# Next layer's adaptive blocks among the mix blocks, semaphores cleared in two parts, norms tile by tile, 64-row pairs side by side

## Chip, cores and metric

The kernel runs on one core of a Trainium2 chip. The metric is the device time in microseconds (us); the median of three runs of the kernel before is 3287.51 us.

## What is computed

The reference is a decoder trunk of two layers for 256 tokens of width 1024. For each layer:

```
ada = silu(c) @ w_ada + b_ada -> shift1, scale1, gate1, shift2, scale2, gate2
h = rms_norm(x) * (1 + scale1) + shift1
z = h @ w_in                     # columns for three mixers and the merge gates
m = sig(gA)*attention(z) + sig(gB)*conformer_conv(z) + sig(gC)*rwkv7(z)
x = x + (1 + gate1) * (m @ w_out)
h = rms_norm(x) * (1 + scale2) + shift2
x = x + (1 + gate2) * peer(h)    # 16384 experts, 16 taken for each token and head
```

and at the end `rms_norm(x)` with a gain. The kernel computes peer() densely: the scores of all 16384 experts, a gate for each (zero for those not taken), and the product of gate times activation with all the rows of v.

## The kernel before

Everything is held transposed, feature by token: x and h are eight tiles of 128 features by 256 tokens (`xT`, `hT`). Weights come as blocks of 1 MB, one after the other, into a ring of four slots (`ring`, `SLOTS`), always in the order of the array `stream`. SyncE's queue (SP) issues nearly all loads from one instruction stream, written out by hand, in which a load of block n waits until block n - 4 has been used up. What SP issues later in this stream waits behind what it issues earlier.

A layer is a loop body (`Fori`), the same program for both layers. Its stages are:

1. Eight adaptive blocks (the columns for shift1 and scale1). VectorE (DVE) reduces each with two tensor_tensor_reduce (L1181) against silu(c). The other 16 adaptive blocks lie further on in the stream, between blocks that TensorE (PE) uses (`late_ada`).
2. The first norm: ScalarE (ACT) squares all of xT in one instruction (L894), PE sums with eight matmuls against ones (`norm_sum`, L553), ACT takes the root (L896), DVE takes the reciprocal (L1133), scales eight tiles (L1136) and adds the shift to eight tiles (L1142).
3. The projection z, each weight split in a high and a low part (`zw_hi` by ACT at L916, `zw_lo` by DVE at L1220), three matmuls for one (L547).
4. Attention, convolution and RWKV. In RWKV, `pairs` (L712, L713) multiplies 64-row operands: a head has 64 rows, and two heads share the 128 partitions. A head's two matmuls (Bh, Kh) follow each other, then come those of the next head. They fill the time in which PE would wait for ACT's copies between the steps of a chain (L758, L769, L788).
5. `W_OUT`, the projection of the merged mixers (L532), all engines meet, then the second norm as in 2.
6. Scores: 64 blocks of u (`PEER`), split in high and low parts, 24 matmuls for each of 128 chunks of experts (L835). The activations are stored to DRAM row by row (`store_act`, L448), as are the gates.
7. Mix: 64 blocks of v, two chunks each. For chunk c, ACT copies the high part of v (`v_high`, L1075, four deep), DVE subtracts for the low part (`v_low`, L1570), and `weigh(c)` multiplies the gate row by the activation row (L1676) and splits the product in high and low (L1680, L1682), two deep. PE does twelve matmuls a chunk (L856) and needs v's low part and the split of the product. In DVE's stream v_low(c+3) and weigh(c+2) take turns.
8. End: ACT and DVE copy the sums out of PSUM, PE transposes them (L881), DVE adds to xT (L1706), the engines meet, and POOL clears all 138 semaphores while the others wait (`layer_end`). Then the next pass of the loop begins with loads of the parameters `prm`, of c and of the first four blocks.

The place that matters for stage 7 is SP's loop. In the kernel before it reads:

```
for q in range(SLOTS, PAIRS):
    sp.wait_ge(S["v_lo"], 2 * (q - SLOTS) + 2)
    load(PEER + PAIRS + q)
    for c in (2 * q - 6, 2 * q - 5):
        if c >= ROWS_DEEP:
            load_rows(c)
```

So when v_low of both chunks of block q - 4 is done (chunks up to 2q - 7), SP loads block q, and then the gate and activation rows of chunks 2q - 6 and 2q - 5, 128 KB each (`load_rows`: L455, L456). DVE waits for the rows of a chunk at L1676.

## Time and profile before

| | us |
|---|---|
| median of three runs (3279.75 to 3289.98) | 3287.51 |
| the profiled execution, its own time | 3290.19 |
| its span, from the first to the last instruction | 3288.4 |
| PE busy in it | 2962.9 (90%) |
| DVE busy | 2314.4 (70%) |
| ACT busy | 1114.9 (34%) |
| POOL busy | 99.0 (3%) |
| HBM traffic, mean over the span | 186 GB/s |

A row of the profile names the engine, the line of the kernel, the operation, and the tiles written and read (out<-in). In square brackets stands how long the engine was idle before, and what ended that wait. L12 is line 12 of the kernel before. Views in order of time begin with the start and the duration in us; a row with "xN" covers N instructions. A matmul in f32 shows as two records. The mean granted clock of TensorE is 0.954 of full speed.

### The profile page before, as it was taken

To read this page: it belongs to the slowest core of one execution; us is meant where nothing else is said; L and a number is where in the kernel's file an instruction comes from. 1 tells how busy PE (TensorE), PEld (TensorE's weight loads), DVE (VectorE), ACT (ScalarE), POOL (GpSimd) and SP (SyncE) were. 2 spreads that over 40 slices of the span, in tenths; PEclk is the share of its full clock that TensorE was granted. 3 is DMA by queue.
4 is the path that set the end of the run, shared out by engine and by line. 5 is a ranking of instruction groups with operands and counts; after the bars stand their busy time and mean duration, and the time that the engine had idled before them with its cause. 6 is when DMAs were issued, how large, how long until landed. Compare 5 with 4: busy or idle time off the path is not lost. (4 is left out here: it accounts for less than half of the span.)

```text
span 3288.4 us, 49870 instructions
## 1 busy us (share of the span) xinstructions
PE 2962.9 (90%) x19180; PEld 2662.7 (81%) x19180; DVE 2314.4 (70%) x4571; ACT 1114.9 (34%) x1532; POOL 99.0 (3%) x120
## 2 busy tenths in 40 slices
PE   4997898879999999999769879897899999999996
PEld 4996787768999998887569858776789999988885
DVE  6888564545887847888578895645468868478885
ACT  3434321201444444333234342211024444433332
POOL 0000003200000000000000000031000000000000
PEclk8998999989999999999979989998999999999998
DMA  6552340053666688887465424300546575978783
GB/s 243 184 188 77 119 170 8 29 208 116 207 208 213 215 295 283 283 280 277 142 238 188 156 77 159 129 8 32 211 139 213 189 249 190 320 266 284 278 281 109
DMA packets 268992, 613.57 MB, mean 187 GB/s; under 512 B 45520, under 2 KB 210000, under 8 KB 211664
## 3 DMA queue, kind: packets, MB, share of 16 engines
q1 hardware_dynamic: 203152, 576.79, 49.9%
q10 hardware_dynamic: 65600, 33.55, 3.4%
q8 instruction: 154, 2.52, 0.3%
q14 instruction: 86, 0.70, 0.1%
HBM read 540.53 MB, written 69.73 MB: 186 GB/s over the span
## 5 line engine op out<-in xcount | busy, mean ns | idle before, releaser
L835 PE MATMUL ps<-h_hi,u_hi 128*128 128x256 f32 x2048 | 592.0, 289 | 34.6 <-DVE u_lo L1563 34.2
L835 PE MATMUL ps<-h_hi,u_lo 128*128 128x256 f32 x2048 | 582.4, 284 | 0.0
L835 PE MATMUL ps<-h_lo,u_hi 128*128 128x256 f32 x2048 | 582.2, 284 | 0.0
L1563 DVE TENSOR_TENSOR u_lo<-ring,u_hi 128x1024 fp32r<-128x1024 f32 x256 | 311.7, 1220 | 252.4 <-ACT u_hi L1067 251.9
L835 PEld LDWEIGHTS ps<-h_hi,u_hi 128*128 128x128 f32 x2048 | 395.5, 193 | 42.9 <-DVE u_lo L1563 36.0
L1075 ACT ACTIVATE v_hi<-ring 128x1024 fp32r<-128x1024 f32 x256 | 271.3, 1062 | 437.8 <-PE ps L856 437.8
L835 PEld LDWEIGHTS ps<-h_lo,u_hi 128*128 128x128 f32 x2048 | 395.5, 193 | 0.0
L835 PEld LDWEIGHTS ps<-h_hi,u_lo 128*128 128x128 f32 x2048 | 395.2, 193 | 0.0
L1570 DVE TENSOR_TENSOR v_lo<-ring,v_hi 128x1024 fp32r<-128x1024 f32 x256 | 313.1, 1224 | 49.3 <-ACT v_hi L1075 44.5
L856 PE MATMUL ps<-v_hi,w_hi 128*128 128x512 f32 x1024 | 323.5, 397 | 4.3 <-DVE w_lo L1682 4.3
L856 PE MATMUL ps<-v_lo,w_hi 128*128 128x512 f32 x1024 | 322.9, 396 | 0.0
L856 PE MATMUL ps<-v_hi,w_lo 128*128 128x512 f32 x1024 | 322.9, 396 | 0.0
L532 PE MATMUL ps<-hT,ring 128*128 128x256 f32 x1280 | 295.5, 391 | 19.1 <-DVE hT L1142 15.9
L532 PEld LDWEIGHTS ps<-hT,ring 128*128 128x128 f32 x1280 | 248.7, 197 | 59.1 <-DVE hT L1142 16.7
L1067 ACT ACTIVATE u_hi<-ring 128x1024 fp32r<-128x1024 f32 x256 | 269.0, 1052 | 0.0
L1082 ACT ACTIVATE region<-ps 128x256 f32<-128x256 f32 x256 | 98.1, 383 | 488.2 <-DMA act_rows<-region 268.0
L532 PE MATMUL ps<-region,ring 128*128 128x256 f32 x1024 | 233.2, 390 | 26.8 <-DVE region L1489 21.1
L532 PEld LDWEIGHTS ps<-region,ring 128*128 128x128 f32 x1024 | 199.9, 196 | 58.0 <-DVE region L1489 21.9
L856 PEld LDWEIGHTS ps<-v_hi,w_hi 128*128 128x128 f32 x1024 | 192.1, 188 | 53.0 <-issue 6.9
L856 PEld LDWEIGHTS ps<-v_lo,w_hi 128*128 128x128 f32 x1024 | 192.8, 188 | 47.1
L856 PEld LDWEIGHTS ps<-v_hi,w_lo 128*128 128x128 f32 x1024 | 192.9, 188 | 47.0
L1243 DVE SCALAR_TENSOR_TENSOR region<-region,prm 128x256 f32<-128x256 f32 x480 | 200.2, 479 | 1.7
(300 smaller groups left out, 4363.0 us busy)
## 6 DMA issues: line engine op xcount, KB each, us to landing
ring<-in_stream SPq DMA_DIRECT2D x444, 1024.0 KB, 5.0
act_rows<-region SPq DMA_DIRECT2D x256, 128.0 KB, 5.5
gate_rows<-region ACTq DMA_DIRECT2D x4, 8192.0 KB, 55.6
region<-gate_rows SPq DMA_DIRECT2D x256, 128.0 KB, 4.6
region<-act_rows SPq DMA_DIRECT2D x256, 128.0 KB, 4.7
region<-in_c SPq DMA_DIRECT2D x6, 512.0 KB, 3.6
xT<-in_x SPq DMA_DIRECT2D x1, 1024.0 KB, 7.9
small_inverses<-route SPq DMA_DIRECT2D x4, 256.0 KB, 2.0
```

Source lines behind the costliest of these rows:

```text
L532: ins = mm(o[:, a, :], w[:, k, a * P:(a + 1) * P], src[:, k, :], start=k == 0, stop=k == KD - 1)
L835: ins = mm(ps[:, c % 4, 0:T], x, y[:, k, :], start=k == 0 and i == 0, stop=k == KD - 1 and i == 2)
L856: ins = mm(ps[:, 4 + 2 * tt + half, :], x, y[:, c % V_DEEP, half * 512:(half + 1) * 512], start=c == 0 and i == 0, stop=c == CHUNKS - 1 an ...
L1067: A(u_hi[:, c % U_DEEP, :], ring[:, n % SLOTS, (c % 2) * D:(c % 2 + 1) * D], ACT.Copy).then_inc(S["u_hi"], 1)
L1075: A(v_hi[:, c % V_DEEP, :], ring[:, n % SLOTS, (c % 2) * D:(c % 2 + 1) * D], ACT.Copy).then_inc(S["v_hi"], 1)
L1082: A(act_s[:, c % 4, :], ps[:, c % 4, 0:T], ACT.Gelu).then_inc(S["s_gelu"], 1)
L1243: ins = vec.scalar_tensor_tensor(cy[:, k, :], upad[:, k, tap:tap + T], V("conv_w", tap * KD + k), cy[:, k, :], ALU.mult, ALU.add)
L1563: vec.tensor_tensor(u_lo[:, c % U_DEEP, :], ring[:, slot, (c % 2) * D:(c % 2 + 1) * D], u_hi[:, c % U_DEEP, :].bitcast(F32), ALU.subtract) ...
L1570: vec.tensor_tensor(v_lo[:, c % V_DEEP, :], ring[:, slot, (c % 2) * D:(c % 2 + 1) * D], v_hi[:, c % V_DEEP, :].bitcast(F32), ALU.subtract) ...
```

## The change

- The eight adaptive blocks of a layer are no longer at its head. Those of the first layer are loaded and reduced ahead of the loop, before anything else but c, the positions and the constants. Those of the next layer stand among the v blocks of the mix: after five v blocks, and then one after each seven. DVE reduces one just ahead of v_low of the first chunk of the v block that follows it (`next_ada`). Both layers do this; the last layer's copies go unused.
- The next layer's prm and first four blocks are loaded during and at the end of the mix, with semaphores of their own (`first_in`).
- Semaphores are cleared in two parts: 94 during the scores, 48 at the layer's end. The engines don't meet at W_OUT's end nor at the layer's end; they pass marks (`layer_past`) and wait for POOL only at the loop's end (`layer_next`).
- Norms go tile by tile: ACT squares two tiles at a time as they become ready, PE begins the second norm's sum ahead of the last W_OUT block, the shift is added by ACT while DVE scales the next tile, the head of layer 2's norm runs while POOL clears, and the output is stored in two halves.
- In RWKV the two heads of a partition pair are issued next to each other (`pairs`).

```diff
-ADA = 0
-Z = ADA + N_ADA
+Z = 0
 Z_CONV, Z_RWKV, Z_QK, Z_V, Z_GATE = Z, Z + 8, Z + 21, Z + 29, Z + 33
...
-BLOCKS = PEER + CHUNKS
+V_FIRST = PEER + PAIRS
+ADA_NEXT = tuple(V_FIRST + 5 + 8 * j for j in range(N_ADA))
+V_AT = tuple(n for n in range(V_FIRST, V_FIRST + PAIRS + N_ADA) if n not in ADA_NEXT)
+BLOCKS = V_FIRST + PAIRS + N_ADA
...
+        cleared_early = [prm_in, *first_in, *diag_out, diag_in, small_out, small_in, ada_used, lora_used, *(S[n] for n in early)]
+        cleared = [c_in, *row_in, *act_out, *landed, used, *bank_read, dve_ch, stage, *(S[n] for n in late)]
...
+        def landing(eng, n):
+            if n < SLOTS:
+                eng.wait_ge(first_in[n], 16)
             else:
-                eng.drain()
-                eng.wait_ge(layer_done, l * 4 + 4)
-                eng.sem_inc(seen, 1)
-                for s in cleared:
-                    eng.sem_clear(s)
-                eng.sem_inc(layer_go, 1)
+                eng.wait_ge(landed[n % SLOTS], 16 * (n // SLOTS))
+
+        def layer_past(eng):
+            eng.drain().then_inc(layer_done, 1)
+
+        def layer_next(eng, l):
+            eng.wait_ge(layer_go, l + 1)
+            eng.sem_inc(seen, 1)
...
+            for j in range(SLOTS, N_ADA):
+                sp.wait_ge(start_steps, 1 + j - SLOTS + 1)
+                start_ada(j)
+            for n in range(SLOTS):
+                sp.wait_ge(start_steps, 1 + N_ADA - SLOTS + n + 1)
+                sp.dma_start(ring[:, n, :], stream[n]).then_inc(first_in[n], 16)
             with sp.Fori(0, DEPTH) as l:
-                sp.dma_start(prm[:, :], prm_dram[l]).then_inc(prm_in, 16)
-                sp.dma_start(c_row1, c_dram).then_inc(c_in, 16)
-                for n in range(SLOTS):
-                    sp.dma_start(ring[:, n, :], stream[l * BLOCKS + n]).then_inc(landed[n], 16)
...
+                sp.wait_ge(S["early_cleared"], 1)
+                sp.dma_start(c_row3, c_dram).then_inc(c_in, 16)
+                sp.dma_start(prm[:, :], prm_dram[l + 1]).then_inc(prm_in, 16)
...
-                for q in range(SLOTS, PAIRS):
-                    sp.wait_ge(S["v_lo"], 2 * (q - SLOTS) + 2)
-                    load(PEER + PAIRS + q)
-                    for c in (2 * q - 6, 2 * q - 5):
-                        if c >= ROWS_DEEP:
-                            load_rows(c)
+                def passed(n):
+                    if n in ADA_NEXT:
+                        sp.wait_ge(S["next_ada"], ADA_NEXT.index(n) + 1)
+                    else:
+                        sp.wait_ge(S["v_lo"], 2 * V_AT.index(n) + 2)
+
+                for n in range(V_FIRST + SLOTS, BLOCKS):
+                    passed(n - SLOTS)
+                    load(n)
+                    if n in V_AT:
+                        q = V_AT.index(n)
+                        for c in (2 * q - 6, 2 * q - 5):
+                            if c >= ROWS_DEEP:
+                                load_rows(c)
                 for c in range(2 * PAIRS - 6, CHUNKS):
                     load_rows(c)
-                layer_end(sp, l)
-            sp.wait_ge(S["normed"], 1)
-            sp.dma_start(out_dram, hT[:, :, :]).then_inc(stored, 16)
-            sp.wait_ge(stored, 16)
+                for n in range(SLOTS):
+                    passed(BLOCKS - SLOTS + (n - BLOCKS) % SLOTS)
+                    sp.dma_start(ring[:, n, :], stream[l * BLOCKS + BLOCKS + n]).then_inc(first_in[n], 16)
+                layer_past(sp)
+                layer_next(sp, l)
...
-                norm_sum(1)
-
-                pe.wait_ge(S["h_ready"], 1)
-                pe.wait_ge(S["zh_hi"], 1)
+                pe.wait_ge(S["zh_hi"], 2)
...
+                def pairs(g, s, left, right):
+
+                    if g == 4:
+                        return
+                    tt, p = s // 4, (4 * g + s % 4) // 2
+                    toks, e = slice(tt * P, (tt + 1) * P), g * GRP + s
+                    if left and e >= 4:
+                        pe.wait_ge(S["pairs_masked"], e - 2)
+                    for key, first, half in ((Bh, left, 0), (Kh, right, T)):
+                        for j in range(2) if first else ():
+                            rows = slice(j * HN, (j + 1) * HN)
+                            ins = mm(ps[:, s % 4 + j, half:half + T], key[rows, p, toks], AR[rows, p, tt, :, :].rearrange("p a b -> p (a b)"),
+                                     start=True, stop=True)
+                            if half:
+                                ins.then_inc(S["pairs_mm"], 1)
...
-                        pairs(g + 1, 4 * tt)
+                        pairs(g + 1, 4 * tt, True, False)
                         pe.wait_ge(S["rhs_copied"], e + 1)
                         for s in range(4):
                             two = rhs_u[:, s // 2 * 2:s // 2 * 2 + 2, :].rearrange("p s i -> p (s i)")
                             ins = mm(ps[:, 7, s * P:(s + 1) * P], XY[:, tt * 4 + s, 1, :], two, start=True, stop=True)
                         ins.then_inc(S["u_mm"], 1)
-                        pairs(g + 1, 4 * tt + 1)
+                        pairs(g + 1, 4 * tt, False, True)
                         if g and tt == 1:
                             pe.wait_ge(S["gn_squares"], g)
...
-                for n in W_OUT:
+                for n in W_OUT[:3]:
                     project(n, merged)
-                st.meet()
-                norm_sum(2)
-                pe.wait_ge(S["h_ready"], 2)
+                norm_sum(1, 0, 4)
+                project(W_OUT[3], merged)
+                norm_sum(1, 4, KD)
+                pe.wait_ge(S["h_ready"], 2 * KD)
+                st.mark()
...
-                for tt in range(TT):
-                    for k in range(KD):
+                for k in range(KD):
+                    for tt in range(TT):
                         ins = nc.tensor.transpose(ps[:, k // 2, k % 2 * T + tt * P:k % 2 * T + (tt + 1) * P], acc[:, tt, k * P:(k + 1) * P], ident)
-                ins.then_inc(S["acc_T"], 1)
-                st.meet()
-                layer_end(pe, l)
-            norm_sum(1)
+                    if k % 2:
+                        ins.then_inc(S["acc_T"], 1)
+                layer_past(pe)
+                norm_sum(0)
+                layer_next(pe, l)
 
...
+                for i, n in enumerate(W_OUT):
+                    was_read(act, n)
+                    square(i)
+                norm_root(1)
+                shift(1)
+                st.mark()
...
+                for i in range(4):
+                    act.wait_ge(S["x_read"], i + 1)
+                    square(i)
+                layer_next(act, l)
...
+                block_lo(Z)
+                modulate(0, gs[:, 0, :], S["h_scaled"])
+                for half in (slice(0, KD // 2), slice(KD // 2, KD)):
+                    dve.wait_ge(S["h_ready"], half.stop)
+                    vec.tensor_copy(zh_hi[:, half, :], hT[:, half, :]).then_inc(S["zh_hi"], 1)
...
+                def next_ada(j):
+
+                    landing(dve, ADA_NEXT[j])
+                    dve.wait_ge(S["next_ada"] if j else S["c_silu"], j or 3)
+                    for a in range(2):
+                        ins = vec.tensor_tensor_reduce(ada_prod3[:, a], ring[:, ADA_NEXT[j] % SLOTS, a * D:(a + 1) * D], c_row3, 1.0, 0.0, ALU.mult, ALU.add,
+                                                       next_acc[:, 2 * j + a:2 * j + a + 1])
+                    ins.then_inc(S["next_ada"], 1)
+
+                ada_at = {2 * (V_AT.index(n + 1)) - 3: j for j, n in enumerate(ADA_NEXT)}
                 v_low(0)
                 weigh(0)
                 v_low(1)
                 weigh(1)
                 v_low(2)
                 for c in range(CHUNKS):
+                    if c in ada_at:
+                        next_ada(ada_at[c])
                     if c + 3 < CHUNKS:
                         v_low(c + 3)
                     if c + 2 < CHUNKS:
                         weigh(c + 2)
+                dve.wait_ge(S["next_ada"], N_ADA)
+                dve.wait_ge(S["early_cleared"], 1)
+                next_gains()
                 dve.wait_ge(S["acc_ready"], 2)
                 vec.tensor_copy(acc[:, 1, :], ps[:, 6:8, :].rearrange("p b n -> p (b n)")).then_inc(S["rest_copied"], 1)
-                dve.wait_ge(S["acc_T"], 1)
+                layer_past(dve)
                 for k in range(KD):
+                    if k % 2 == 0:
+                        dve.wait_ge(S["acc_T"], k // 2 + 1)
                     ins = vec.scalar_tensor_tensor(xT[:, k, :], ps[:, k // 2, (k % 2) * T:(k % 2 + 1) * T], gate1[:, 1, k:k + 1],
                                                    xT[:, k, :], ALU.mult, ALU.add)
-                ch.join(ins)
-                st.meet()
-                layer_end(dve, l)
+                    if k % 2:
+                        ins.then_inc(S["x_read"], 1)
+                layer_next(dve, l)
...
-                for _ in range(3):
-                    st.meet()
-                layer_end(pool, l, clears=True)
+                st.meet()
+                st.mark()
+                pool.wait_ge(stage, 4 * st.k)
+                pool.wait_ge(S["loads_past"], 1)
+                for one in cleared_early:
+                    pool.sem_clear(one)
+                pool.sem_inc(S["early_cleared"], 1)
+                pool.drain()
+                pool.wait_ge(layer_done, l * 4 + 4)
+                pool.sem_inc(seen, 1)
+                for one in cleared:
+                    pool.sem_clear(one)
+                pool.sem_inc(layer_go, 1)
```

Three places show the new order. The first is SP in the mix. Around a v block load before (any of them, the pattern repeats; an ISA row is the wait for `v_lo`, L444 loads the ring, L455 and L456 the rows):

```order
L444 ISA [waits v_lo]
L444 DMA ring<-in_stream 128x2048
L455 DMA region<-gate_rows 128x256 [waits act_stored0,w_raw]
L456 DMA region<-act_rows 128x256
L455 DMA region<-gate_rows 128x256 [waits act_stored1,w_raw]
L456 DMA region<-act_rows 128x256
```

And now, where an adaptive block stands in the stream (L470 loads the ring, L481 and L482 the rows):

```order
L470 ISA [waits v_lo]
L470 DMA ring<-in_stream 128x2048
L470 ISA [waits v_lo]
L470 DMA ring<-in_stream 128x2048
L481 DMA region<-gate_rows 128x256 [waits act_stored0,w_raw]
L482 DMA region<-act_rows 128x256
L481 DMA region<-gate_rows 128x256 [waits act_stored1,w_raw]
L482 DMA region<-act_rows 128x256
```

The first load is the adaptive block and has no rows behind it. The v block behind it, and the two after that, wait for the block four places back in the stream, which is now three v blocks back and not four.

The second is DVE in the mix, where an adaptive block is reduced (L1770; L1643 is v_low, L1749, L1753 and L1755 are weigh). Before, the row that ends with `w_hi]` was followed at once by that with `v_hi]`:

```order
L1755 TENSOR_TENSOR w_lo<-hot,w_hi 128x256 [waits w_hi]
L1770 ISA region,next_acc<-ring,region 128x1024 [waits next_ada,block_landed3]
L1770 ISA next_acc 128x1
L1770 ISA region,next_acc<-ring,region 128x1024
L1770 ISA next_acc 128x1
L1643 TENSOR_TENSOR v_lo<-ring,v_hi 128x1024 [waits v_hi]
L1749 TENSOR_TENSOR hot<-region 128x256 [waits rows_landed3]
```

Two reductions of 128x1024 stand ahead of v_low there; nothing else in DVE's mix has moved.

The third is PE at the end of W_OUT (L532 and L578 are projections, L553 and L600 the sum of squares). Before:

```order
L532 MATMUL ps<-region,ring 128x256 [waits bank_read0,block_landed0]
L532 MATMUL ps<-region,ring 128x256 x15
L553 MATMUL ps<-region,cst 128x256 [waits squares,stage_done]
L553 MATMUL ps<-region,cst 128x256 x7
L532 MATMUL ps<-hT,ring 128x256 [waits bank_read1,block_landed2,h_ready]
```

Now:

```order
L600 MATMUL ps<-region,cst 128x256 [waits squares]
L600 MATMUL ps<-region,cst 128x256
L600 MATMUL ps<-region,cst 128x256 [waits squares]
L600 MATMUL ps<-region,cst 128x256
L578 MATMUL ps<-region,ring 128x256 [waits bank_read0,block_landed0]
L578 MATMUL ps<-region,ring 128x256 x15
L600 MATMUL ps<-region,cst 128x256 [waits squares]
L600 MATMUL ps<-region,cst 128x256
L600 MATMUL ps<-region,cst 128x256 [waits squares]
L600 MATMUL ps<-region,cst 128x256
L578 MATMUL ps<-hT,ring 128x256 [waits h_ready,bank_read1,block_landed2]
```

Four of the eight sums stand ahead of the last projection, and none waits for a meeting.

## Rows read from the trace of the kernel before

**Rows 1.** The chain that ended last, in order of time: its longest piece, in the mix
```profile
2932.63 320.86 PE ps L856 x1368
```

**Rows 2.** In order of time, the start: first adaptive reduction, first weight split, first projection
```profile
19.16 1.23 DVE L1181 CUSTOM_DVE_ANT_0 region<-ring,region 128x1024 f32<-128x1024 f32 x1 [1.28 <-ACT region L905]
...
37.32 1.91 ACT L916 ACTIVATE zw_hi<-ring 128x2048 fp32r<-128x2048 f32 x1 [9.08 <-DMA ring<-in_stream]
...
50.28 2.05 PE L547 MATMUL ps<-zh_hi,zw_hi 128*128 128x256 f32 x8 [24.07 <-DVE zw_lo L1220]
```

**Rows 3.** In order of time, from the first layer's last mix matmul to the second's projection
```profile
1619.66 0.64 PE L856 MATMUL ps<-v_hi,w_lo 128*128 128x512 f32 x2
...
1623.68 3.22 DVE L1706 SCALAR_TENSOR_TENSOR xT<-ps,gate,xT 128x256 f32<-128x256 f32 x8 [2.12 <-PE ps L881]
...
1641.12 1.28 ACT L905 ACT_TABLE_LOAD   x1 [21.17 <-issue]
...
1681.46 2.05 PE L547 MATMUL ps<-zh_hi,zw_hi 128*128 128x256 f32 x8 [24.75 <-DVE zw_lo L1220]
```

**Rows 4.** In order of time, the end of the program
```profile
3270.51 1.91 ACT L894 ACTIVATE region<-xT 128x2048 f32<-128x2048 f32 x1 [17.38 <-POOLq L415]
...
3284.13 0.34 SPq L511 DMA_DIRECT2D out<-hT  x1
```

**Rows 5.** In order of time, the second norm of the second layer
```profile
2355.36 0.88 DVE L1549 SCALAR_TENSOR_TENSOR xT<-ps,gate,xT 128x256 f32<-128x256 f32 x2 [3.41 <-PE ps L532]
...
2358.37 5.38 PE L553 MATMUL ps<-region,cst 128*128 128x256 f32 x16 [3.12 <-ACT region L894]
...
2366.15 3.25 DVE L1136 SCALAR_TENSOR_TENSOR hT<-xT,gs,rstd 128x256 f32<-128x256 f32 x8
...
2371.68 16.24 PE L532 MATMUL ps<-hT,ring 128*128 128x256 f32 x64 [7.94 <-DVE hT L1142]
```

**Rows 6.** In order of time, DVE alone, two chunks of the mix
```profile
3102.74 1.23 DVE L1570 TENSOR_TENSOR v_lo<-ring,v_hi 128x1024 fp32r<-128x1024 f32 x1 [0.39 <-ACT v_hi L1075]
3104.23 0.42 DVE L1676 TENSOR_TENSOR hot<-region 128x256 f32<-128x256 f32 x1 [0.27 <-DMA region<-act_rows]
...
3108.36 1.23 DVE L1570 TENSOR_TENSOR v_lo<-ring,v_hi 128x1024 fp32r<-128x1024 f32 x1 [0.39 <-ACT v_hi L1075]
3109.68 0.42 DVE L1676 TENSOR_TENSOR hot<-region 128x256 f32<-128x256 f32 x1
...
3110.54 0.42 DVE L1682 TENSOR_TENSOR w_lo<-hot,w_hi 128x256 fp32r<-128x256 f32 x1
```

**Rows 7.** In order of time, SP's queue alone, the same two chunks
```profile
3104.14 0.34 SPq L444 DMA_DIRECT2D ring<-in_stream  x1
...
3105.01 0.42 SPq L456 DMA_DIRECT2D region<-act_rows  x1
```

**Rows 8.** In order of time, ACT alone, the same two chunks
```profile
3107.27 1.06 ACT L1075 ACTIVATE v_hi<-ring 128x1024 fp32r<-128x1024 f32 x1 [1.75 <-PE ps L856]
```

**Rows 9.** Transfers from act_rows in the mix, 2940 to 3250 us: issue to landing
```profile
DMA to landing us min/median/max: 2.1/4.7/6.2
```

**Rows 10.** In order of time, DVE alone, early in the second layer's mix
```profile
2901.79 0.42 DVE L1676 TENSOR_TENSOR hot<-region 128x256 f32<-128x256 f32 x1 [3.38 <-DMA region<-act_rows]
```

**Rows 11.** In order of time, PE behind its longest gap in RWKV
```profile
2135.52 2.04 PE L736 MATMUL ps<-region,hT 128*128 128x128 f32 x8 [5.00 <-POOL region L1734]
```

**Rows 12.** Windows of time: us, busy us (and records) by engine, granted clock, DMA share, GB/s
```profile
2136.00:2140.00 4.00, 3.74 (x18) 3.47 (x17) 0.00 (x0) 0.68 (x2) 2.96 (x5) 0.50 0.00 0
```

**Rows 13.** In order of time, two 64-row matmuls of different rows in the convolution's stage
```profile
2018.93 0.48 PE L628 MATMUL ps<-region,ring 64*128 64x256 f32 x1
...
2018.93 0.48 PE L629 MATMUL ps<-region,ring 64*128 64x256 f32 x1
```

**Rows 14.** In order of time, a single head of `pairs` between two steps of the chain
```profile
2167.70 0.70 PE L712 MATMUL ps<-region 64*128 64x256 f32 x2
...
2168.76 1.16 PE L769 MATMUL ps<-hT,region 128*128 128x128 f32 x8
```

More of the change, by code:

```diff
@@ L548, in project_split, with norm_sum @@
                 ins.then_inc(used, 1)
-            def norm_sum(count):
-                pe.wait_ge(S["squares"], count)
-                for k in range(KD):
+            def norm_sum(turn, first=0, last=KD):
+                for k in range(first, last):
+                    if k % 2 == 0:
+                        pe.wait_ge(S["squares"], 4 * turn + k // 2 + 1)
                     ins = mm(ps[:, 4, 0:T], ones, sqx[:, k, :], start=k == 0, stop=k == KD - 1)
-                ins.then_inc(S["sumsq"], 1)
+                if last == KD:
+                    ins.then_inc(S["sumsq"], 1)
             def total_sum(src, i):
@@ L718, in gn_sums @@
                     ins.then_inc(S["gn_mm"], 1)
-                pairs(0, *range(GRP))
+                for s in range(0, GRP, 2):
+                    pairs(0, s, True, True)
                 for g in range(4):
```

255 lines of the change are left out of this document (136 added, 119 removed).

## The prediction

> **What bounds the kernel now.** I read the chain that ended last first. Its longest piece is the mix: 1368 matmuls of PE in one unbroken run of 320.86 us [rows 1], 12 for each chunk, so 114 chunks at 2.81 us. There PE is the bound, and all else only has to keep up. The views in order of time then show what is left between such runs. At the start PE first multiplies for the projection at 50.28 [rows 2]. From the end of the first layer's mix at 1620.30 to the projection at 1681.46 PE has little to do for 61.2 us [rows 3]. The program goes on for 34.9 us behind its last mix matmul, which ends at 3253.49 [rows 1, 4]. A second norm holds PE for 16.4 us, from 2355.3 to 2371.68 [rows 5]. The change is aimed at these four places, some 180 us in all.
>
> The third thing to read is who keeps up in the mix, and by how much, since eight blocks are added there. In DVE's rows a chunk takes v_low 1.23, weigh 0.42, and two splits; DVE is the engine nearest to PE. One of its waits is no wait for an engine: at 3104.23 it ends with the transfer of the activation row, after 0.27 us [rows 6]. That is the row to look at. SP issued a block load at 3104.14, right behind the v_low that ended at 3103.97, and the activation row at 3105.01 [rows 6, 7]. By SP's loop these are the rows that weigh takes after two more v_lows, at 3109.68 [rows 6]. The median row lands 4.7 us behind its issue [rows 9], at 3109.7. So rows arrive just as they are needed, 5.7 us behind the v_low that lets SP go on, and two chunks last 5.62 us. There is nothing to spare.
>
> **The gains.** I sum against the profiled execution, 3290.2.
>
> *Start.* Adaptive reductions began at 19.16 and, 16 of them at 1.2 us, ended near 38.5; the first block of z was being split at 37.32 [rows 2]. Now c, positions and constants land first, the rope steps end some 3 us earlier, and the eight blocks follow without the pause in which the ring stood full. The first z block was behind nine blocks and x at 37.3; I take about 4 us less. DVE's shift of 2.3 us (2369.40 to 2371.68 [rows 5]) becomes 0.5 of ACT's, and a cast is halved (0.7, by the size alone). DVE's split goes ahead of the norm, so it is off the end but waits for the block's landing; I count nothing for it. Sum: -6.5, between -3 and -10.
>
> *First layer's end.* From the mix's end T: the transposes let DVE add to the first tiles at T+1.9, but PE's mark comes when they are done, at T+3.4 (1623.68 less 1620.30). POOL then clears 48 semaphores in place of 138. DVE's last addition ends at T+6.6 (1626.90), so at 3260.1 in the second layer; the clearing of 138 took from there until 3270.51 [rows 4], 10.4 us, so 48 take 3.6. In the first layer it took until 1641.12 [rows 3], 14.2, so going round the loop costs 3.8 more. ACT starts the z split at T+10.8, 1.9 us; root with its table load (1.3 [rows 3]) until T+14.5; DVE's split until T+15.1, reciprocal 1.8, eight scalings 3.3 [rows 5], last shift 0.5, half a cast 0.7: PE at T+21.4 instead of T+61.2. That is -39.8, between -35 and -44.
>
> *Last layer's end.* The same up to the root, without the way round the loop: norm's sum at T+7.4, root at T+9, reciprocal T+11, scalings T+14.4, and the second half's store, 3.1 us (4.3 for the whole [rows 4], less half a megabyte at the pace of 1.2). T+17.5 against T+34.9: -17.4, between -14 and -19.
>
> *Second norm.* Behind the last projection: additions 0.9, squares of two tiles 0.6 (a quarter of 1.91 [rows 4], and a start), two sums of the eight that took 5.38 [rows 5], but the table load of 1.3 in the meantime is longer, root and reciprocal 2.4 (2363.75 to 2366.15), scalings 3.3, last shift 0.5: 9.1 us instead of 16.4. Four of the sums, 0.67 each in that row and some 0.44 in a PE that is warm, now stand ahead of the last projection: +1.7. So -5.6 a layer, -11.2 for both, between -8 and -14.
>
> *64-row pairs.* A single head holds PE for 1.06 us between two steps [rows 14]. Where two matmuls of different rows are neighbours they start at the same 2018.93 and end together [rows 13]. Issued like that, half the work takes 0.63, and the chain's next step is ready by then. That is -0.43 at two places for each of 6 group halves and 2 layers: -10, between 0 and -13.
>
> Together -85: without a new cost the kernel would come to 3205.
>
> **The cost in the mix.** The reductions themselves: two in DVE, 2.4 us, eight times a layer. From the row at 3110.54 the split of a chunk's product ends at 3110.96 [rows 6]. PE needs it when it has done the chunk before: ACT's v_high at 3107.27 starts when a chunk ends [rows 8], so the next two end at 3110.04 and 3112.85, and the slack is 1.9 us. DVE idles 0.4 us a chunk at v_low [rows 6], so 2.4 late is made up for within a few chunks. The cost is between 0 and 0.5 each.
>
> The ring costs more. SP loads block n when block n - 4 is passed. Of any four places one may now hold an adaptive block, which has no rows of its own. So for the three v blocks behind each adaptive block the block four back is v block q - 3 and no longer q - 4: SP goes on only when v_low(2q-5) is done, and then loads block q and the rows of chunks 2q-6 and 2q-5. But DVE's next instruction behind v_low(2q-5) is weigh(2q-6), and that waits for just these rows. The 5.7 us from v_low to the rows that two chunks hid lie open. Say L = 5.7.
>
> - First such block: weigh starts L behind v_low instead of 0.1. The split is late by 5.6, of which PE's slack takes 1.9: PE stands for 3.7.
> - Second and third: from weigh to the next wait DVE needs weigh 1.2, v_low 1.15, weigh 1.2, v_low 1.2 (from 3109.68 to 3110.96, and the 1.23, with little between), in all 4.75, and then L. A block lasts 10.45 in place of 5.62: 4.8 each, 9.7.
> - Then the adaptive block. Count from the third late weigh: its split is ready at 1.3 and PE works until 4.1. DVE reduces until 3.7, v_low until 4.85, weigh until 6.1: PE stands for 2.0, and works until 8.9.
> - The fourth block waits for the reduction, at 3.7. Its rows come at 3.7 + L = 9.4, the split at 10.6: PE stands for 1.7.
>
> Sum 3.7 + 9.7 + 2.0 + 1.7 = 17.1 us for each adaptive block. Then three v blocks go normally and DVE, 0.4 us a chunk faster than PE, regains its slack. 8 blocks, 2 layers (the second layer's copies are of no use, but cost the same): **+273 us**.
>
> What the rows show of such a wait: early in the mix, where rows were late for another reason, DVE stood 3.38 us for an activation row [rows 10]. Bounds on L: the fastest row landed in 2.1 us and the slowest in 6.2 [rows 9], each 1.04 behind the v_low, so 3.1 to 7.2. With L = 3.1 the sum is 1.2 + 4.5 + 2.0 = 7.7 a block, +123; with 7.2 it is 5.2 + 12.7 + 2.0 + 3.2 = 23.1, +370. I take the median, since a late row still stands behind its 1 MB block in the queue as it does now; with less traffic 5.2 is as good, which makes 15 and +240.
>
> The Trainium skill has for one DMA about 2.0 us and the bytes at 436 GB/s ("DMA: Bandwidth & Descriptors", Anatomy of one DMA; fitted on GpSimd's path). An estimate by that page, for the block and the two rows ahead of the second: 2.0 + 3.0 us behind the first issue, L = 5.2. By it an adaptive block costs 15 and the sum is 33 us less, 3442; the rows 6 and 9, which decide for me, have 5.7.
>
> The early loads of c and prm in SP's stream and the Silu between ACT's v_highs (a table load and 1.1 us, with 1.75 us idle a chunk [rows 8]) I cost at nothing; without that cover 2 to 3 us each a layer. Clearing 94 semaphores during the scores is POOL's, which is idle there.
>
> 3290.2 - 85 + 273 = 3478 by the profiled execution. The median of the runs shown is 2.7 lower: **3475**.
>
> **Rivals.**
>
> *Rows are hidden anyway.* If they came before weigh asks for them, only the gains and the reductions would be left: 3290 - 85 + 3 less 2.7 = 3205, faster than before. It decides at the point where an adaptive block costs 85/16 = 5.3 us, which is L = 2.3. For it: nothing is asked of PE, and the fastest row landed in 2.1 [rows 9]. Against it: the smallest landing and the two issues make 3.1. Chance 0.08.
>
> *Rows come quicker.* With a quieter queue L is 3.1 to 4.5, and the time 3325 to 3400. Against it: the queue is not full now either; what fills the 4.7 is mostly the block ahead. Chance 0.12.
>
> *The clock falls as well.* Behind 5.00 us of idling eight matmuls took 2.04 us [rows 11], and the granted clock of 2136 to 2140 is 0.50, the level of 1.2 GHz [rows 12]. The late blocks have gaps of 3.7 to 4.8 us. Where a gap ends at half clock, a chunk takes up to 5.6 us; two fill 11.2 of 10.45. Inside the late blocks that is nearly hidden by the waits. At the fourth block it is not: if three chunks run at the half clock there, 8 us more for each adaptive block, +130, 3605. For it speaks the gap in rows 11; against it, that most of PE's losses fall where it waits anyway. Chance 0.08.
>
> The page's rule is the same (the Trainium skill, "TensorE: Matmul & The Clock Gate", HAM oscillation): gaps of waiting for DMA between bursts put each burst at the half clock. By that rule this rival is the forecast, with 3605.
>
> *The joints give less.* If POOL's clearing, table loads or the way round the loop take the gains of the two ends by half, 3475 + 29 = 3504; inside the range.
>
> **Numbers.** The forecast with its own spread (L from 5.2 to 6.2, joints as bounded) has 0.72, 3430 to 3520. The range for 8 in 10 reaches toward the quick rows on one side and the clock on the other: 3395 to 3560. This kernel's measurement can tell about 0.3% from no change, 10 us. Slower has 0.72 + 0.12 + 0.08, less 0.02 for a mix of the last rival with small L: 0.90. Faster 0.08, the same 0.02.
>
> **What would show it.** In the profile after, DVE's waits at the product of the rows (L1749) ended by act_rows would sum to some 300 us, with 24 of 5 to 6 us in each layer's mix, in threes after each reduction L1770; the mix would last about 137 us longer a layer. PE should start the projection near 44 at the start, some 21 us after the first mix ends, and the store end 17 to 18 us after the last. The forecast is wrong if those waits are short or absent, and wrong in size if they last 3 us, or if PE's granted clock in the mix stands at 0.5 for long.

## The result and the profile after

The changed kernel takes 3489.94 us (median of 4 runs, 3486.73 to 3491.89), against 3283.63 for the kernel before, run beside it. The ratio is 1.0626, with a 95% interval from 1.0602 to 1.0649: it is 6.3% slower. Its profiled execution took 3491.89, its span is 3490.1.

The windows of time between the marks that the prediction named give the whole account. First the kernel before (us, busy us and records of PE, PEld, DVE, ACT and POOL, granted clock, DMA share, GB/s):

```profile
50.28:1258.00 1207.72, 1107.76 (x8015) 1032.38 (x8016) 826.58 (x1702) 406.98 (x626) 49.05 (x56) 0.96 0.47 162
1258.00:1620.30 362.30, 360.64 (x1538) 288.79 (x1536) 290.57 (x508) 133.09 (x126) 0.00 (x0) 1.00 0.76 266
...
1681.46:2890.20 1208.74, 1111.97 (x8014) 1035.62 (x8015) 827.72 (x1704) 407.34 (x626) 49.03 (x56) 0.96 0.47 162
2890.20:3253.49 363.29, 360.60 (x1538) 288.79 (x1536) 289.70 (x506) 133.07 (x126) 0.00 (x0) 1.00 0.76 265
```

And the changed kernel, from its first projection to its end:

```profile
45.19:1241.30 1196.11, 1097.52 (x8014) 1022.61 (x8015) 825.57 (x1698) 416.02 (x642) 49.28 (x56) 0.96 0.48 164
1241.30:1747.66 506.36, 405.61 (x1538) 313.63 (x1537) 302.66 (x540) 135.10 (x128) 0.00 (x0) 0.91 0.60 214
1747.66:1768.76 21.10, 5.66 (x33) 4.68 (x33) 12.97 (x22) 10.27 (x16) 0.34 (x2) 0.73 0.04 12
1768.76:2964.00 1195.24, 1098.55 (x8015) 1024.13 (x8016) 825.24 (x1697) 416.07 (x642) 49.31 (x56) 0.96 0.48 164
2964.00:3472.93 508.93, 408.00 (x1538) 315.06 (x1536) 303.11 (x542) 135.10 (x128) 0.00 (x0) 0.91 0.60 213
3472.93:3490.10 17.17, 5.66 (x33) 4.68 (x32) 9.46 (x18) 4.28 (x6) 0.00 (x0) 0.84 0.17 69
```

The first number behind a stretch is its length. The two mixes went from 362.30 and 363.29 us to 506.36 and 508.93. The joint between the layers is 21.10 long where it was 61.2 [rows 3], the end 17.17 where it was 34.9 [rows 1, 4], and the stretches from projection to mix are 11.6 and 13.5 shorter. With 5.1 at the start (45.19 against 50.28 [rows 2]) that makes -5.1 - 11.6 + 144.1 - 40.1 - 13.5 + 145.6 - 17.7 = +201.7, the difference of the two spans.

What DVE waits for in the first mix, longest sum first (us in total, times, longest):

```profile
DVE hot L1749 <- DMA region<-act_rows: 169.3, 47, 6.4
```

The second mix has 171.1 more. The prediction asked for some 300 in both; it is 340.4, of which 49.4 were there in the kernel before, in 95 waits of at most 3.4. The waits of over 5 us are 24 in each layer, in threes, 5.66 to 6.38 long. Where they lie, DVE alone, in the last group of the first layer:

```profile
1652.25 1.23 DVE L1643 TENSOR_TENSOR v_lo<-ring,v_hi 128x1024 fp32r<-128x1024 f32 x1 [0.39 <-ACT v_hi L1145]
1659.27 0.42 DVE L1749 TENSOR_TENSOR hot<-region 128x256 f32<-128x256 f32 x1 [5.79 <-DMA region<-act_rows]
...
1662.80 1.22 DVE L1643 TENSOR_TENSOR v_lo<-ring,v_hi 128x1024 fp32r<-128x1024 f32 x1
1669.84 0.43 DVE L1749 TENSOR_TENSOR hot<-region 128x256 f32<-128x256 f32 x1 [5.83 <-DMA region<-act_rows]
...
1680.34 0.42 DVE L1749 TENSOR_TENSOR hot<-region 128x256 f32<-128x256 f32 x1 [5.76 <-DMA region<-act_rows]
...
1681.54 1.22 DVE L1770 CUSTOM_DVE_ANT_0 region<-ring,region 128x1024 f32<-128x1024 f32 x1
...
1689.77 0.43 DVE L1749 TENSOR_TENSOR hot<-region 128x256 f32<-128x256 f32 x1 [2.39 <-DMA region<-act_rows]
```

and SP's queue alone (the first row holds two issues, the second of them at its end, 1653.99):

```profile
1648.03 5.96 SPq L470 DMA_DIRECT2D ring<-in_stream  x2
1654.10 0.37 SPq L481 DMA_DIRECT2D region<-gate_rows  x1
...
1655.68 0.43 SPq L482 DMA_DIRECT2D region<-act_rows  x1
```

This is the pattern of the prediction, in its order. v_low (L1643) ends at 1653.48, and only then does SP issue the block and, from 1654.10, the rows for which DVE has been standing since 1653.5. DVE's next instruction, the product of the rows (L1749), starts at 1659.27, 5.79 late. Two more follow, 10.57 and 10.50 us apart (the prediction had 10.45), then the reductions (L1770), and a fourth wait of 2.39. Against that, [rows 6, 7] show the same issue at 3104.14 with two chunks of work between it and the product. What PE makes of it:

```profile
1660.70 0.71 PE L911 MATMUL ps<-v_hi,w_hi 128*128 128x512 f32 x2 [4.02 <-DVE w_lo L1755]
...
1671.27 0.71 PE L911 MATMUL ps<-v_hi,w_hi 128*128 128x512 f32 x2 [3.17 <-DVE w_lo L1755]
...
1673.24 1.05 PE L911 MATMUL ps<-v_hi,w_hi 128*128 128x512 f32 x2
...
1681.77 0.71 PE L911 MATMUL ps<-v_hi,w_hi 128*128 128x512 f32 x2 [3.11 <-DVE w_lo L1755]
...
1683.09 1.05 PE L911 MATMUL ps<-v_hi,w_lo 128*128 128x512 f32 x2
...
1691.20 0.71 PE L911 MATMUL ps<-v_hi,w_hi 128*128 128x512 f32 x2 [1.76 <-DVE w_lo L1755]
```

PE stands 4.02, 3.17 and 3.11 us for the three late blocks and 1.76 for the fourth. The matmuls in between (a row is two of them) last 1.05 in place of 0.63 for a while after each of the three long gaps. From the third late block's first matmul to the fourth's it is 9.43, and no gap lies between them until the last 1.76.

### The profile page after: what moved, and what is told of

It is laid out like the page before. It is cut to its first block and busy times, and to the rows that moved or that the text cites. A ratio compares the mean times of both kernels' runs of the same rounds, so it can differ in the third digit from the quotient of the medians.

```text
span 3490.1 us, 49922 instructions
## 1 busy us (share of the span) xinstructions
PE 3026.4 (87%) x19180; PEld 2689.0 (77%) x19180; DVE 2311.2 (66%) x4573; ACT 1129.8 (32%) x1580; POOL 99.5 (3%) x120
## 5 line engine op out<-in xcount | busy, mean ns | idle before, releaser
L911 PE MATMUL ps<-v_hi,w_hi 128*128 128x512 f32 x1024 | 361.5, 437 | 201.7 <-DVE w_lo L1755 201.3
L911 PEld LDWEIGHTS ps<-v_hi,w_hi 128*128 128x128 f32 x1024 | 207.4, 210 | 278.6 <-issue 233.6
L911 PE MATMUL ps<-v_lo,w_hi 128*128 128x512 f32 x1024 | 348.9, 424 | 0.0
L911 PE MATMUL ps<-v_hi,w_lo 128*128 128x512 f32 x1024 | 346.3, 421 | 0.0
L1749 DVE TENSOR_TENSOR hot<-region 128x256 f32<-128x256 f32 x256 | 107.7, 421 | 340.6 <-DMA region<-act_rows 340.4
L1643 DVE TENSOR_TENSOR v_lo<-ring,v_hi 128x1024 fp32r<-128x1024 f32 x256 | 312.2, 1220 | 22.7 <-ACT v_hi L1145 21.9
L578 PE MATMUL ps<-hT,ring 128*128 128x256 f32 x1280 | 299.1, 395 | 17.0 <-ACT hT L959 13.0
L578 PEld LDWEIGHTS ps<-hT,ring 128*128 128x128 f32 x1280 | 251.2, 199 | 57.5 <-issue 16.5
L578 PE MATMUL ps<-region,ring 128*128 128x256 f32 x1024 | 233.8, 390 | 25.4 <-DVE region L1562 19.8
L911 PEld LDWEIGHTS ps<-v_lo,w_hi 128*128 128x128 f32 x1024 | 211.7, 207 | 54.1
L911 PEld LDWEIGHTS ps<-v_hi,w_lo 128*128 128x128 f32 x1024 | 209.8, 205 | 53.1
L578 PEld LDWEIGHTS ps<-region,ring 128*128 128x128 f32 x1024 | 200.1, 196 | 57.3 <-DVE region L1562 21.2
```

Of the source, the lines that this page charges most:

```text
L578: ins = mm(o[:, a, :], w[:, k, a * P:(a + 1) * P], src[:, k, :], start=k == 0, stop=k == KD - 1)
L911: ins = mm(ps[:, 4 + 2 * tt + half, :], x, y[:, c % V_DEEP, half * 512:(half + 1) * 512], start=c == 0 and i == 0, stop=c == CHUNKS - 1 an ...
L1643: vec.tensor_tensor(v_lo[:, c % V_DEEP, :], ring[:, slot, (c % 2) * D:(c % 2 + 1) * D], v_hi[:, c % V_DEEP, :].bitcast(F32), ALU.subtract) ...
L1749: vec.tensor_tensor(w, a_row[:, c % ROWS_DEEP, :], c_row[:, c % ROWS_DEEP, :], ALU.mult).then_inc(S["w_raw"], 1)
```

## The experiments

Each run was timed beside the kernel before. Its median there was 3284.3 for experiments 1 to 4, 3285.6 for 5 to 8, and 3283.6 for 9 to 11 and the second run of 5.

**1. Rows first.** In the changed kernel SP issues the rows ahead of the wait for the block four back:

```diff
 for n in range(V_FIRST + SLOTS, BLOCKS):
-    passed(n - SLOTS)
-    load(n)
     if n in V_AT:
         ...
                 load_rows(c)
+    passed(n - SLOTS)
+    load(n)
```

> The changed kernel, but SP issues the rows of two chunks ahead of the wait for the block four back, not behind it. Theory A (the rows wait for the wrong v_low): the waits of DVE for act_rows go from 340 us to below 20, each mix lasts 363 to 368 us in place of 506 and 509, and the time is 3200 to 3215. Theory B (the eight added blocks load the queue, or their reductions load DVE): the mix keeps most of its length, 3400 or more.

Measured: 3211.24 us (3205.48 to 3216.98), ratio 0.9769 (0.9736 to 0.9801). The adaptive blocks still come, 1 MB each, and are still reduced. The mixes last 371.3 and 369.5, above the 363 to 368 that I expected. DVE's wait in the first of them:

```profile
DVE hot L1749 <- DMA region<-act_rows: 16.5, 17, 2.9
```

The two mixes had grown by 290 us. With the place of the issue alone all but 15 of them are gone, and these 15 are all that is left for Theory B, that bytes or reductions are the cost. The waits for rows add up to 31.6 in both layers, not below 20, since one pair of rows in a group still stood behind an adaptive block's load (experiment 5 moves that one too).

**2. The same wait, but the rows ahead of the block.** The order is `passed`, rows, `load`.

> The changed kernel, but behind the unchanged wait SP issues the rows of two chunks first and the block of 1 MB behind them. Theory A with a row held up by the block ahead of it: it lands some 2.1 to 3.1 us behind its issue, the waits are 3 to 4 us long in place of 5.8, and the time is 3330 to 3385. If a row takes its 4.7 us whatever is ahead of it: 3470 to 3495.

Measured: 3303.96 us (3300.94 to 3307.10), ratio 1.0060 (1.0039 to 1.0081): below what I expected, by more than its spread. The median transfers, issue to landing, in most of the first mix, of the changed kernel and then of this one:

```profile
ring<-in_stream SPq DMA_DIRECT2D x63, 1024.0 KB, 4.9
...
region<-act_rows SPq DMA_DIRECT2D x110, 128.0 KB, 4.7
```

```profile
ring<-in_stream SPq DMA_DIRECT2D x61, 1024.0 KB, 6.1
...
region<-act_rows SPq DMA_DIRECT2D x108, 128.0 KB, 2.7
```

A row of 128 KB takes 4.7 us behind a block and 2.7 ahead of it. The three waits of a group, DVE alone:

```profile
1299.75 0.42 DVE L1749 TENSOR_TENSOR hot<-region 128x256 f32<-128x256 f32 x1 [3.12 <-DMA region<-act_rows]
...
1307.55 0.43 DVE L1749 TENSOR_TENSOR hot<-region 128x256 f32<-128x256 f32 x1 [3.05 <-DMA region<-act_rows]
...
1314.84 0.42 DVE L1749 TENSOR_TENSOR hot<-region 128x256 f32<-128x256 f32 x1 [2.55 <-DMA region<-act_rows]
```

They are 3.12, 3.05 and 2.55 in this group; the mean of all 48 is 2.7, in place of 5.8. The mixes last 414.8 and 414.1, so a group costs 103.3 / 16 = 6.5 us more than in the kernel before, where the changed kernel pays 18.1. Put through the prediction's steps, L = 2.7 gives 0.7 for the first late block, 3.7 for the next two, 2.0 at the adaptive block and nothing at the fourth, 6.4 in all. So the sum holds at this delay too. What I had too high for this run was the delay: 3 to 4 us, and the waits are 2.7.

**3. Late rows in the kernel before.** No adaptive block, no reduction, no byte more. In 24 places a layer, the same as in the changed kernel, SP waits one v block longer:

```diff
-sp.wait_ge(S["v_lo"], 2 * (q - SLOTS) + 2)
+sp.wait_ge(S["v_lo"], 2 * (q - SLOTS + (q % 7 in (5, 6, 0) and 5 <= q <= 56)) + 2)
```

> The kernel before, without any adaptive block in the mix; only in the 24 places a layer where the changed kernel has it so, SP waits for v block q - 3 in place of q - 4. Theory A: 13.4 us (PE's waits alone) to 15.5 us (with the slower clock behind them) for each of 16 groups of three: 3284 + 215 to 250 = 3500 to 3535, slower than the changed kernel, which has its gains beside. Theory B: nothing is added to queue or DVE, so 3284 to 3300.

Measured: 3534.43 us (3524.49 to 3542.99), ratio 1.0748 (1.0713 to 1.0784). The wait alone makes the kernel before slower than the changed one. Its mixes last 491.7 and 487.5, 15.85 us more for each group of three, where the prediction's steps for three late blocks have 13.4.

**4. Without the reductions, rows late.**

> The changed kernel without the two reductions of each adaptive block (left out: the next layer's adaptive sums; a copy of two columns stands in their place, the block still lands). Theory A: the late rows stay; only the 2.4 us of DVE between the third and the fourth block go, 2 to 2.5 us of some 18 for each adaptive block: 3445 to 3465. If the reductions were the cost: 3300 or less.

Measured: 3455.34 us (3453.97 to 3459.10), ratio 1.0520 (1.0490 to 1.0550), as Theory A has it: 2.2 us less for each of 16 adaptive blocks. Its mixes last 493.6 and 489.1, so a group still costs 16.1 us without any reduction.

**5. Rows ahead of every block.** SP issues the rows of the next v block before the load of an adaptive block too. It was run twice (the old places of `load_rows`, behind `load(n)`, are taken out, which is not shown):

```diff
 for n in range(V_FIRST + SLOTS, BLOCKS):
+    q = V_AT.index(n if n in V_AT else n + 1)
+    for c in range(rows_past, 2 * q - 4):
+        load_rows(c)
+    rows_past = max(rows_past, 2 * q - 4)
     passed(n - SLOTS)
     load(n)
```

> The changed kernel with the rows of the next two chunks issued ahead of every block load, ahead of that of an adaptive block too (with the rows only ahead of their own block one pair in each group still came 1.2 to 1.5 us late, and the mixes lasted 371 and 369 us). Theory A: the last waits for rows go, the mixes last 363 to 366 us, and the time is 3198 to 3208. If what is left in the mix is the reductions' cost: no change against the rows ahead of their own block, 3208 to 3215.

> The kernel with rows always first once more, on the same chip as the one with the halves apart, for the comparison of the two: 3200 to 3208.

Measured: 3202.66 (3201.65 to 3209.92), ratio 0.9757 (0.9734 to 0.9780), and again 3204.82 (3200.46 to 3207.58), 0.9758 (0.9745 to 0.9772). DVE's waits for rows in the first mix:

```profile
DVE hot L1749 <- DMA region<-act_rows: 9.2, 13, 2.5
```

The mixes are 367.6 and 367.4 in the first of the two runs, a little longer than expected, and 365.1 and 366.3 in the second. That is 2.8 to 5.3 us longer than before the change. This is the time that the prediction's sum without the cost of the mix has: 3290.2 - 85, less 2.7, is 3202.5.

**6. The semaphores in one part again.** The base here and in 7, 8 and 10 is experiment 5. Of the 94 that are cleared early, 79 go behind the last mark:

```diff
-cleared_early = [prm_in, *first_in, *diag_out, diag_in, small_out, small_in, ada_used, lora_used, *(S[n] for n in early)]
...
+joint = early[:10]
+cleared_early = [prm_in, *first_in, *(S[n] for n in joint)]
...
```

> The kernel with rows always first, but 79 of the 94 semaphores that are cleared early are cleared behind the last engine's mark again, 127 there in place of 48. If the clearing is what the two joints wait for: 79 at 0.075 us, 6 us at each joint, so 12 us slower than with rows always first. If the norm's sums or the last additions end later than the clearing: 0 to 4 us.

Measured: 3220.62 us (3217.43 to 3227.28), ratio 0.9809 (0.9786 to 0.9832). The joint is 27.3 long in place of 21.2 and the end 22.8 in place of 17.1: 6.1 and 5.7, the expected 6 each. The medians differ by 18. In the profiles the rest lies mainly in the stretches from projection to mix (1197.1 and 1194.0 against 1193.8 and 1189.8), from which the edit only takes clearing by POOL away. They scatter by that much: in nine profiles of the same code there the first is 1192.4 to 1197.8 long.

**7. Single heads again.** `pairs` as before, one head at a time:

> The kernel with rows always first, with the 64-row products of RWKV's pairs issued one head at a time as before (the convolution's stage stays with its two abreast). If pairs abreast carry the gain of the stage: 10 (the prediction's term) to 16 us slower (by the traces that stage is 8 us a layer shorter). If the gain comes from elsewhere in it: 0 to 4 us.

Measured: 3216.51 us (3211.15 to 3216.89), ratio 0.9792 (0.9771 to 0.9814), 14 more by the medians and 6 more by the profiled executions. The stage itself, from the first pair to the last product of it, is read below, with the clock.

**8. Without the reductions, rows in time.**

> The kernel with rows always first, without the two reductions of each adaptive block (left out: the next layer's adaptive sums, a copy of two columns in their place). The prediction's 0 to 0.5 us for each of 16: 0 to 8 us faster than with rows always first. If DVE is the bound there: 2.4 us each, up to 38 us faster.

Measured: 3192.87 us (3192.28 to 3196.29), ratio 0.9726 (0.9705 to 0.9747): 10 us less, 0.6 for each adaptive block, just above the bound of 0.5. The mixes are 362.2 and 361.4, no longer than in the kernel before (362.3 and 363.3): no cost of the 1 MB of each adaptive block is seen there once the rows come in time.

**9. A warm TensorE in the late blocks.** The changed kernel with useless matmuls where PE stands:

```diff
+for _ in range(warm.get(c, 0)):
+    mm(ps[:, 3, 0:T], ones, xT[:, 0, :], start=True, stop=True)
 pe.wait_ge(S["v_lo"], c + 1)
 pe.wait_ge(S["w_split"], c + 1)
```

> The changed kernel (rows late as in it), with useless matmuls of TensorE (128x256 f32 into a free bank, about 0.44 us each, 7 before each of the three late chunks of a group and 4 before the fourth) in the time in which it would stand. The changed kernel's mixes have 99 to 100 us of standing and 405.6 to 408 busy against 360.6 before: 45 us a layer of slower clock. If DVE and the rows set the pace in the late blocks, the slower clock lies mostly inside the waits and its loss is the 1 us a group by which the measured 18.1 exceed the forecast's 17.1: 3470 to 3485. If the slower clock adds itself to the waits: 45 us a layer come back, 3400 to 3420.

Measured: 3494.27 us (3489.85 to 3494.70), ratio 1.0643 (1.0627 to 1.0659). Nothing comes back, not even the 16 us that I expected; the mixes last 510.3 and 506.0, against 506.4 and 508.9. The granted clock over the first mix is 0.99 where it was 0.91, so the edit did what it should:

```profile
1239.00:1749.50 510.50, 461.27 (x1940) 366.15 (x1938) 303.11 (x542) 135.14 (x128) 0.00 (x0) 0.99 0.60 213
```

PE alone, in the group that is shown above of the changed kernel:

```profile
1657.97 3.18 PE L906 MATMUL ps<-xT,cst 128*128 128x256 f32 x14
1662.39 0.70 PE L913 MATMUL ps<-v_hi,w_hi 128*128 128x512 f32 x2 [1.23 <-DVE w_lo L1758]
1662.93 0.63 PE L913 MATMUL ps<-v_lo,w_hi 128*128 128x512 f32 x2
...
1688.34 0.71 PE L913 MATMUL ps<-v_hi,w_hi 128*128 128x512 f32 x2 [1.57 <-DVE w_lo L1758]
```

Behind the useless matmuls (L906) the real ones last 0.63 at once. But PE then has the adaptive block to wait for: it stands 1.57 before 1688.34. In the changed kernel there is no gap at this place; the slow matmuls behind 1681.77 fill it. DVE and the rows set the pace in both.

**10. The two halves of a reduction apart.** Base is experiment 5; each half comes behind a chunk of its own:

```diff
-ada_at = {2 * (V_AT.index(n + 1)) - 3: j for j, n in enumerate(ADA_NEXT)}
+ada_at = {2 * V_AT.index(n + 1) - 3 + a: (j, a) for j, n in enumerate(ADA_NEXT) for a in range(2)}
```

> The kernel with rows always first, with the two reductions of an adaptive block behind different chunks (one of 1.2 us each, within PE's slack of 1.9, in place of 2.4 us at once). If the once-only lateness of DVE is what the reductions cost (leaving them out gave 10 us): 3193 to 3199. If their sum is what counts: 3200 to 3206 as with both at once.

Measured: 3201.44 us (3193.91 to 3206.09), ratio 0.9753 (0.9740 to 0.9767). By the times this is no difference from 3204.82. The profiles see more: the mixes are 363.2 and 361.0 long, much as without any reduction (362.2 and 361.4), where the eight mixes of experiment 5 (twice), 6 and 7, with both halves at once, are 364.8 to 367.9. What PE waited for in the first mix, with both halves at once, without reductions, and with the halves apart:

```profile
PE ps L911 <- DVE w_lo L1755: 5.1, 9, 1.6
```

```profile
PE ps L911 <- DVE w_lo L1755: 1.2, 2, 0.6
```

```profile
PE ps L911 <- DVE w_lo L1755: 1.8, 4, 0.6
```

5.1, 1.2 and 1.8 us. In these traces the cost was that DVE is late by 2.4 us at once, and not the sum of its work; whether the kernel is faster by it, 5 runs don't show.

**11. One late pair in a group.** Experiment 3 with one late place in each group in place of three.

> The kernel before, with SP's wait for v block q - 3 only at the first of each of the 16 groups of three. The prediction's first step: 5.6 late less PE's slack of 1.9, 3.7 us for each, +59; with the slower clock behind the gap not hidden here, some 2.4 us more each, +98: 3343 to 3383. If the cost were the same for each late block (246 us over 48 in the run with three late): 5.1 each, 3366. If a single late pair were caught up: below 3310.

Measured: 3382.36 us (3370.67 to 3389.94), ratio 1.0309 (1.0291 to 1.0327). The mixes are 409.3 and 411.6, so 5.96 us for each. PE alone, at one of them:

```profile
1311.90 0.98 PE L856 MATMUL ps<-v_hi,w_hi 128*128 128x512 f32 x2 [4.04 <-DVE w_lo L1682]
...
1313.54 1.05 PE L856 MATMUL ps<-v_hi,w_lo 128*128 128x512 f32 x2
...
1316.32 0.63 PE L856 MATMUL ps<-v_hi,w_hi 128*128 128x512 f32 x2
```

It stands for 4.04 where the first step of my sum had 3.7. Then it works at the slow clock until about 1315.9: the way from 1311.90 to 1316.32 takes 4.42, where six steps of 0.47 are 2.8. These are 1.6 of the other 1.9. Here DVE has its rows and catches up, so nothing hides the slow matmuls. What the second and third late blocks add is read from experiment 3: (15.85 - 5.96) / 2 = 4.9 each, forecast 4.8.

## Why the prediction was right, point by point

**The wait in SP.** The changed kernel has it in three v blocks behind each adaptive block. Shown by experiments 1 and 3 from both sides: with the issue moved the time goes away, and with nothing but the later wait it comes. L was forecast at 5.7; the 48 long waits are 5.8 in the mean.

**The sum for an adaptive block.** Forecast 17.1, measured 289.7 / 16 = 18.1. In the group that is shown, the first gap is 4.02 for the forecast's 3.7. The second and third late blocks last 10.57 and 10.50 in place of 5.62, 9.8 more together, for 9.7. From the third to the fourth it is 9.43, 3.8 more, for 2.0 + 1.7. These make 17.7; what the other 0.4 are was not tried. The reductions' share was measured by itself: without them a group costs 16.1 (experiment 4), 2 less.

One thing in this agreement is luck. The sum has no term for slow matmuls behind the third late block. Where no reduction follows there, they cost: 15.85 for three late blocks in experiment 3, against 13.4, which is 2.4 more. In the changed kernel they fall into the 2.0 for which PE would have stood at the adaptive block (experiment 9 shows that gap open again, 1.57 long). That the two would cover each other the prediction had not worked out.

**The clock.** The gaps did put TensorE at its slower level (1.2 GHz), as [rows 11, 12] had it (the eight records there are four matmuls, not eight; the granted clock of 0.50 is what shows the level). PE is busy 405.6 us in the mix for work that took 360.6. The rival priced that at up to 8 us a group. It priced it where the fourth block would be slow; there the gap is 1.76 long, and the matmuls behind it last 0.63. The slow matmuls of the three late blocks lie in time in which PE would have waited for DVE. The rival named them as nearly hidden, and experiment 9 shows them as worth nothing. Experiment 11 shows the other side: with one late block alone the slow matmuls do cost their 1.6 us. The oscillation rule of the Trainium skill ("TensorE: Matmul & The Clock Gate", HAM oscillation) is seen in the granted clock here (0.91 over the mix, 0.59 from 1681.7 to 1685.6), and its cost only where nothing else was late.

**Rows come quicker, rows hidden.** Neither held. "DMA: Bandwidth & Descriptors" (the Trainium skill, Anatomy of one DMA) gave an estimate of 5.2 for L; 5.8 was measured, and that decides. I had written that what fills a row's 4.7 us is mostly the block ahead. Experiment 2 makes it 2.0 of them, less than half.

**Joint and end.** Forecast -39.8 and -17.4, measured -40.1 and -17.7. ACT's split of the first z block, the root and PE in the joint, in order of time:

```profile
1758.23 1.91 ACT L979 ACTIVATE zw_hi<-ring 128x2048 fp32r<-128x2048 f32 x1 [4.53 <-issue]
...
1761.45 0.47 ACT L954 ACTIVATE rstd<-ps,cst 128x256 f32<-128x256 f32 x1
...
1768.76 1.57 PEld L593 LDWEIGHTS ps<-zh_hi,zw_hi 128*128 128x128 f32 x7 [14.04 <-DVE zh_hi L1268]
```

T is 1747.66. The split was forecast at T + 10.8 and starts at T + 10.6, the root ends at T + 14.3 (14.5), PE starts at T + 21.1 (21.4). That the clearing sets this place is shown by experiment 6, 0.075 us for each semaphore.

**Start.** -5.1 for -6.5, with the first projection at 45.19. Which of its parts was short I did not try.

**The second norm.** The last sums and PE behind them, in the second layer:

```profile
2427.88 7.07 PE L578 MATMUL ps<-region,ring 128*128 128x256 f32 x32
...
2436.65 1.13 PE L600 MATMUL ps<-region,cst 128*128 128x256 f32 x4 [0.83 <-ACT region L950]
2444.28 6.28 PE L578 MATMUL ps<-hT,ring 128*128 128x256 f32 x14 [6.50 <-ACT hT L959]
```

The last projection ended at 2434.9, so PE is held for 9.3 us (forecast 9.1).

**The pairs.** Forecast -5 a layer. The whole stage is 9.8 shorter, and there are two reasons, one of which I had not seen. The kernel before, the stage of the second layer and 10 us within it:

```profile
2125.70:2274.80 149.10, 129.99 (x1010) 114.11 (x1011) 73.79 (x120) 26.50 (x51) 49.03 (x56) 0.93 0.03 5
2155.70:2165.70 10.00, 9.97 (x64) 7.77 (x64) 6.07 (x15) 1.15 (x3) 2.35 (x4) 0.66 0.08 28
```

The changed kernel, and the same 10 us:

```profile
2213.70:2353.00 139.30, 118.02 (x1010) 102.83 (x1011) 73.25 (x120) 26.70 (x51) 49.31 (x56) 0.98 0.03 5
2243.70:2253.70 10.00, 9.80 (x94) 7.77 (x94) 7.19 (x18) 1.54 (x4) 3.86 (x5) 1.00 0.08 28
```

And with single heads (experiment 7), both layers:

```profile
487.30:629.70 142.40, 123.27 (x1011) 108.17 (x1012) 73.96 (x120) 26.48 (x51) 49.15 (x56) 0.98 0.03 5
2073.20:2219.40 146.20, 127.12 (x1010) 111.96 (x1011) 73.97 (x120) 26.48 (x51) 49.12 (x56) 0.95 0.03 5
```

The granted clock of the stage is 0.93 before and 0.98 after. In the ten microseconds that are shown it was 0.66 before and is 1.00, and it is 1.00 at that place with single heads too. Single heads gave 142.40 in a layer without such a drop and 146.20 in one with drops (0.95). So the heads abreast are worth 3 us a layer where the clock is alike (142.4 against 139.4), and 6.8 of the 9.8 come with the clock or with what else the change does in front of this stage; these two were not told apart. The prediction's 5 was too large for the one and knew nothing of the other.

**What was given back.** Up to the first matmul of the key scores (L818 before, L873 after) the two layers are 16.8 and 13.9 us shorter. From there to the mix they took 507.3 and 502.8 us, where it was 502.1 and 502.5, and so 5.2 of the first layer's are lost again. The same code took 497.8 to 507.7 there in the two layers of nine profiles, so this need not have a cause in the change, and the 11.6 and 13.5 (forecast 10.6 each) are known no better than that.

**The total.** By the profiled execution 3491.9 against 3478, 14 more: 16.7 in the mixes, -3 in all else.

## What to carry to other kernels

When one in-order queue issues two kinds of transfers, ask for each kind which event lets it go, not only for the one whose slots you count. Here an inserted block without rows moved the rows' trigger from one v_low to the next but one, right in front of the instruction that needed them. The edit that mends it (experiment 5) changes only the order in which SP waits and issues, and turns 3490 into 3203, 2.4% faster than the kernel before.

A gap that made TensorE slow cost something here only where TensorE was what was waited for next: nothing in experiment 9, some 1.6 us a gap in experiment 11. Price it after the waits, not beside them.

## What was not expected of the hardware

A transfer of 128 KB behind one of 1 MB in the same queue landed after 4.7 us, ahead of it after 2.7. The block then took 6.1 in place of 4.9 (rows of experiment 2): part of the delay is moved to it, where nobody waits.

In RWKV's stage the granted clock fell to 0.66 in the kernel before, in both layers at the same place, without any gap of PE over 1.4 us in the 15 us ahead of it. With two heads abreast it did not fall there. It did not fall there with single heads either, in experiment 7 (1.00 in both layers), so the order of the heads is not shown to be the cause. What it was that it fell for, these runs don't show.
